# A hybrid SSD, differential-attention and PEER block on one core: ScalarE's queue reordered, and one of four stream buffers turned into a place for gathered rows

## What is computed

```python
hn = rmsnorm(x); z, xbc, dt, q, k, v = split(hn @ w_in)
x = x + concat([ssd(z, xbc, dt), diff_attention(q, k, v)]) @ w_out     # 4 heads, 2 maps a head
xb = rmsnorm(x)                                                        # then PEER
q  = (xb @ w_q).reshape(tokens, 8, 2, 128)
sc = einsum('thjd,hjnd->thjn', q, sub_keys)                            # 8 heads x 2 x 128 keys
idx, g = top-16 of the 256 sums of the two top-16, softmax             # 16 of 16384 experts a head
h  = gelu(einsum('td,thkd->thk', xb, u[idx]))                          # rows of u
x  = x + einsum('thk,thkd->td', g * h, v[idx])                         # rows of v
```

## Time and profile before

| | |
|---|---|
| median of 3 runs | 1404.65 us (1404.16 to 1406.03) |
| profiled execution | 1406.21 us |
| its span | 1403.3 us |
| mean granted clock | 0.995 |
| TensorE, VectorE, ScalarE, GpSimd busy | 1372.8, 1085.2, 435.1, 612.7 us |
| DMA | 467.69 MB, mean 333 GB/s |

### The profile page before, as it was taken

One profiled execution on the slowest core, in us unless ns is written; L12 is line 12 of the kernel. 1 busy time (PEld: TensorE's weight loads), 2 busy tenths in 40 slices (PEclk: granted clock), 3 DMA queues, 4 the chain that ended last, 5 costly groups with the idle time before them and its releaser, 6 DMA issues.

```text
span 1403.3 us, 16312 instructions
## 1 busy us (share of the span) xinstructions
PE 1372.8 (98%) x5402; PEld 937.3 (67%) x5402; DVE 1085.2 (77%) x2469; ACT 435.1 (31%) x1219; POOL 612.7 (44%) x516
## 2 busy tenths in 40 slices
PE   7999999998999999999999999999999999999998
PEld 5656648566488888888899999885444444444443
DVE  4535445898899999999988998998777667765665
ACT  2533532544412121112777887772000000000000
POOL 0000001732855444434457566654577646644440
PEclk9999999999999999999999999999999999999999
DMA  8322334974999999988899999999999999999997
GB/s 304 141 110 105 119 142 176 370 286 162 411 379 408 389 337 378 326 299 320 300 400 378 398 389 383 388 376 366 384 410 409 409 409 409 410 409 409 410 409 313
DMA packets 121619, 467.69 MB, mean 333 GB/s; under 512 B 13760, under 2 KB 14144, under 8 KB 115008
## 3 DMA queue, kind: packets, MB, share of 16 engines
q0 software_dynamic: 73728, 268.47, 49.5%
q1 hardware_dynamic: 47520, 197.66, 36.6%
q10 hardware_dynamic: 288, 0.52, 0.1%
HBM read 462.67 MB, written 3.93 MB: 333 GB/s over the span
## 4 chain that ended last, share of the span: by engine, by line
PE 52%; DVE 24%; DMA 12%; issue 7%; POOL 3%; ACT 2%; SPq 0%; DVEq 0%; ACTq 0%
PE BANKS L944 31%; PE BANKS L722 11%; DMA UV<-v,IDX 8%; DVE X L1611 7%; PE BANKS L714 6%; DMA UV<-u,IDX 4%; POOL UV L1653 3%; DVE BIG L1422 2%; DVE BIG L1606 2%; DVE UV L1606 2%; DVE BIG L1414 2%; DVE BIG L1416 1%; DVE SMALL L1419 1%; DVE BIG L1437 1%; DVE SMALL L1411 1%
## 5 line engine op out<-in xcount | busy, mean ns | idle before, releaser
L1653 POOL DMA_INDIRECT UV<-u,IDX x153 | 187.9, 1228 | 409.9 <-DVE IDX L1483 264.8
L1653 POOL DMA_INDIRECT UV<-v,IDX x159 | 191.5, 1204 | 121.7 <-DVE X L1611 52.9
L1611 DVE SCALAR_TENSOR_TENSOR X<-UV,HG,X 128x1024 f32<-128x1024 f32 x159 | 204.1, 1283 | 39.8 <-DMA UV<-v,IDX 37.3
L920 PE MATMUL BANKS<-T 128*128 128x256 f32 x1024 | 229.1, 379 | 0.0
L944 PE MATMUL BANKS<-T,BIG 128*128 128x512 f32 x512 | 226.9, 596 | 2.0 <-DVE BIG L1627 2.0
L944 PE MATMUL BANKS<-Y,BIG 128*128 128x512 f32 x512 | 225.1, 592 | 0.0
L1606 DVE SCALAR_TENSOR_TENSOR UV<-UV,Y 128x1024 f32<-128x1024 f32 x153 | 186.6, 1223 | 48.7 <-DMA UV<-u,IDX 47.5
L920 PE MATMUL BANKS<-T,Y 128*128 128x256 f32 x992 | 221.9, 379 | 0.0
L920 PEld LDWEIGHTS BANKS<-T 128*128 128x128 f32 x1024 | 192.0, 190 | 24.7
L920 PEld LDWEIGHTS BANKS<-T,Y 128*128 128x128 f32 x992 | 186.0, 190 | 24.0
L944 PEld LDWEIGHTS BANKS<-T,BIG 128*128 128x128 f32 x512 | 97.7, 191 | 125.5 <-issue 122.1
(11 more groups left out here) (272 smaller groups left out, 1248.4 us busy)
## 6 DMA issues: line engine op xcount, KB each, us to landing
T<-u_t SPq DMA_DIRECT2D x64, 512.0 KB, 6.6
T<-v SPq DMA_DIRECT2D x64, 512.0 KB, 6.8
Y<-v SPq DMA_DIRECT2D x64, 512.0 KB, 6.8
Y<-u_t SPq DMA_DIRECT2D x62, 512.0 KB, 6.7
BIG<-w_in SPq DMA_DIRECT2D x23, 1024.0 KB, 6.9
BIG<-w_q SPq DMA_DIRECT2D x16, 1024.0 KB, 8.0
BIG<-w_out SPq DMA_DIRECT2D x8, 1024.0 KB, 6.8
UV<-v,IDX POOLq DMA_INDIRECT x159, 8.2
```

The source lines that it names most:

```text
L920: last = nc.tensor.matmul(PS[(i + 2) % 4][:, 0:HT], ub[:, c, :], T8[:, 1, c, :], start=(c == 0), stop=(c == KC - 1))
L1611: stt(xb, row, HG[:, n % 2, i % UNIT:i % UNIT + 1], xb, ALU.mult, ALU.add).then_inc(used, 1)
L1653: pool.indirect_dma_start(row_place(s), None, u if kind == "ru" else v, bass.IndirectOffsetOnAxis(IDX[:, b, c:c + 1], 0)).then_inc(row_in[ ...
```

## The change

Four things are edited. ScalarE's exponentials become a step `E` of their own for maps 8 to 15 (TensorE and VectorE keep step `A`): E 8 after both first masks, E i+1 after copy B i, E 15 after W 14's copy and ahead of N 2's root. The dense norm F 3 comes before U 2, and ScalarE's copies of key products 6 and 7 (`kc`) after U 3; W 16 and W 17 write banks 2 and 3. `STREAM` loses Y[3], so NS = 3, only load 2 of u goes to X, and load 5 waits for the keys in Y[2]. Y[3] becomes a standing place for gathered rows from row `rows_until(("K", 15)) + 14` on, opened when key product 15 is done.

```diff
     def second_attention(first, end, after, between):
-        out = on("m A", first) + on("m A", first + 1) + between[:1] + on("c", first) + between[1:]
+        out = on("m A", first) + on("m A", first + 1) + on("E", first) + between[:1] + on("c", first) + between[1:]
         for i in range(first, end):
             out += on("B", i)
+            if first < i + 1 < end - 1:
+                out += on("E", i + 1)
             if i + 1 < end:
                 out += on("c", i + 1)
...
             if i == 13:
-                out += then[:1] + on("N", 2) + then[1:2] + on("n2", 2) + on("C", i) + then[2:]
+                out += then[:1] + on("E", 15) + on("N", 2) + then[1:2] + on("n2", 2) + on("C", i) + then[2:]
...
-    after[15] += rows(4) + on("F", 2) + rows(1) + on("R1 Q", 3) + many("K", 4, 6) + on("U", 2) + on("F", 3) + many("K", 6, 8) + on("U", 3) + rows(7)
+    after[15] += rows(4) + on("F", 2) + rows(1) + on("R1 Q", 3) + many("K", 4, 6) + on("F", 3) + on("U", 2) + many("K", 6, 8) + on("U", 3) + many("kc", 6, 8) + rows(7)
...
         STREAM = [T8[:, 0, 0:4, :].rearrange("p c n -> p (c n)"), T8[:, 0, 4:8, :].rearrange("p c n -> p (c n)"),
-                  Y[:, HB, :], Y[:, HB + 1, :]]
+                  Y[:, HB, :]]
...
-            return X[:, j, :] if j in (2, 3) else STREAM[j % NS]
+            return X[:, j, :] if j == 2 else STREAM[j % NS]
...
+                if s == rows_until(("K", 15)) + RING + MORE + 1:
+                    free.append(STANDING)
+                    opened[STANDING] = (ks_full, 16)
...
-        w_bank = lambda i: 0 if PH <= i < 2 * PH else i % 2
+        w_bank = lambda i: 0 if PH <= i < 2 * PH else i % 2 + 2 * (i in (16, 17))
...
-                if j in (2, 3):
+                if j == 2:
                     sp.wait_ge(x_away, 16)
...
-                if j in (6, 7):
-                    sp.wait_ge(ks_full, 12 if j == 6 else 16)
+                if j == 5:
+                    sp.wait_ge(ks_full, 12)
...
-                elif step == "A":
+                elif step == "A" and i < 2 * DH or step == "E":
...
-                elif step == "K":
+                elif step == "kc" or step == "K" and i not in (6, 7):
```

More of the change, by code:

```diff
@@ L391, in block_program @@
         used, h_ready, gelu_done = sem("used"), sem("h_ready"), sem("gelu_done")
-        row_in = [sem(f"row_in{i}") for i in range(RING + MORE)]
+        row_in = [sem(f"row_in{i}") for i in range(RING + MORE + 1)]
         sel_ready, selt_full, selt_done = sem("sel_ready"), sem("selt_full"), sem("selt_done")
@@ L450, in spaces @@
                     for m in range(MORE)]
-        SPACES = spaces()
+        SPACES, STANDING = spaces(), RING + MORE
         LAST_IN = {}
         def ring_places():
-            free, found, count, last_in = list(range(RING)), [], [0] * (RING + MORE), {}
+            free, found, count, last_in = list(range(RING)), [], [0] * (RING + MORE + 1), {}
             left, now, opened = [list(sp) for sp in SPACES], [None] * MORE, {}
             for s, step in enumerate(ROWSEQ):
+                if s == rows_until(("K", 15)) + RING + MORE + 1:
+                    free.append(STANDING)
+                    opened[STANDING] = (ks_full, 16)
                 for m in range(MORE):
@@ L472, in ring_places @@
                 count[k] += 1
-                at = now[k - RING][0] if k >= RING else None
+                at = now[k - RING][0] if RING <= k < STANDING else None
                 found.append((k, count[k], last_in.get(k), at, opened.pop(k, None)))
@@ L489, in row_place @@
             k, _, _, at, _ = PLACES[s]
-            return UV[:, k, :] if k < RING else BIG[:, at:at + DM]
+            return UV[:, k, :] if k < RING else Y[:, HB + 1, :] if k == STANDING else BIG[:, at:at + DM]
         def q_at(half, hj):
@@ L890, in _ @@
                         n = weights_in()
-                    channels(half, j, n, bank_01(w_bank(i), q2_done, i + 1), q2_full,
+                    channels(half, j, n, PS[w_bank(i)] if w_bank(i) > 1 else bank_01(w_bank(i), q2_done, i + 1), q2_full,
                              [(ut_done, 4 * half + 3 + c) for c in range(2)])
```

## The result

The changed kernel took **1432.17 us** (median of 4 runs, 1429.46 to 1436.57), the kernel before 1404.41 (1403.18 to 1406.03) beside it. The ratio is 1.0196, with a 95% interval of 1.0170 to 1.0222: 27.8 us slower. The forecast was 1424.9 in a range of 1405 to 1438, with 0.81 on slower. The direction and the main mechanism came as forecast; one term of the sum, that of the v stream, was 8.5 us too small.

The account below looks back on a forecast made before the run. TensorE, 98% busy, was taken as the bound, with VectorE and full DMA engines close behind. Terms -3.3 - 1.0 - 1.7 + 8 + 6.0 - 1.3 + 13.5 = +20.2 on 1404.65 gave 1424.9 us, range 1405 to 1438.

Parts of the forecast that it names:

- v stream: v products, 987 to 1385 us: three buffers cover 6.65 us of a 6.8 us landing; stalls cost +13.5 us.
- ScalarE's order in attention: Second attention half, 296 to 348 us: moved exponentials cut VectorE's own idle time; -3.3 us.
- Dense norm: 378 to 393 us: F3 before U2, key copies after U3, so W16 starts earlier; -1.0 us.
- Clock after W16: The half-clock stretch after 393 us costs 3.1 us; half of it taken as saved, -1.7 us.
- u stream: u products without one-hots, to 678 us: three buffers leave loads too little time; +8 us.
- Turn: From u to v products: the first v loads go out later and hold TensorE up; +6.0 us.
- sixth place: One more slot for gathered rows from 457 us removes most VectorE waits, little TensorE idling; -1.3 us.
- The part for v3: Within the turn: load v3, issued when v0 is finished, lands too late for its product; +3.6 us.
- The end: TensorE's work in order sets the end; VectorE's gathered rows end 2 us before it.
- Rival A: Loads stay hidden, landing at 6.4 us or less; only the turn costs 1: 1398.4 us, chance 0.13.
- Rival B: Late loads' stalls let TensorE's clock fall to half; +10 to 17 us, some 1438 us, chance 0.12.
- Rival C: Late loads belong only to that trace; v +4, u +3, turn +4: 1408.4 us, chance 0.13.

Follow-up runs that it names:

- h4: Kernel before with four buffers, each u load waiting for one product more; 1411.21 us, ratio 1.0050.
- e1: Kernel before with ScalarE's whole reorder alone (exponentials, dense norm, key copies, banks), four buffers, five standing places; 1400.37 us, ratio 0.9975.
- p1: Kernel before with only ScalarE's exponentials in the new order; 1402.02 us, ratio 0.9998.
- p3: Kernel before with ScalarE's whole reorder, the same kernel as e1 measured again; 1399.86 us, ratio 0.9968.
- p2: Kernel before with only the dense norm's order, the copies of keys 6 and 7 and the banks; 1402.50 us, ratio 1.0003.
- e4: Kernel before with four buffers, each v load from the fifth on waiting for one product more; 1422.55 us, ratio 1.0126.
- e2: Kernel before with three stream buffers, the fourth's place idle, ScalarE's order and five standing places as before; 1433.42 us, ratio 1.0222.
- e3: Changed kernel without the sixth standing place (Y[3] idle); 1433.08 us, ratio 1.0215.
- h3: Changed kernel measured again, nothing altered; 1433.78 us, ratio 1.0200.
- h1: Changed kernel with each 512 KB load of u and v in two 256 KB halves; 1454.42 us, ratio 1.0343.
- h2: Kernel of e1 (four buffers, five places) with each load of u and v in two halves; 1441.60 us, ratio 1.0253.

## Why the prediction was right, and where it was off

- **ScalarE's order in attention, forecast -3.3, measured -2.66.** Near in size, only in part right in cause. h4 splits it: with the old order, but without the half clock at 328, R0 comes 1.4 us sooner; the order itself is worth 1.2. The forecast read VectorE's wait for mask 15 (0.8) and part of the wait for N2's root as ScalarE's order; they were the half clock that follows the 2.56 us gap: in h4, VectorE's waits are 1.8 (one of them) for the maximum's input and 1.2 for N2's root, where the earlier trace rows have 2.6 (two) and 1.8. It counted that clock at nothing, because TensorE does not set the end of this stage; but the slow matmuls feed VectorE. This rests on h4's one trace. VectorE's waits of the changed kernel from 296 to 348 us:

```profile
DVE RS L1569 <- ACT NSQ L1121: 0.9, 1, 0.9
DVE RS L1554 <- ACT BIG L1104: 0.9, 1, 0.9
```

  What was left of the wait for N2's root is 0.9 us, as worked out. The second row, at 298.74, is new: with both masks first, VectorE waits 0.9 us for map 8's exponentials, where the forecast left 0.2. So 4.4 us of waits became 1.8, which is the 2.66. The two gaps of TensorE went as forecast, but gaps of 1.25 (at 340.44) and 1.55 (at 345.43, ahead of R0) took their place.
- **Dense norm, forecast -1.0, measured -0.98.** Right, and the same within 0.02 in all eight traces of the new order.
- **Clock after W16, forecast -1.7, measured -3.1** between these two executions: the midpoint of an open question, and the 3.1 is no fixed price. Over the eight traces of the new order the clock fell in three, and where it fell for 3.4 us, in either order, the 64 records took 15.45 to 15.74, 1.4 to 1.7 more than 14.05; only the profile before had 6.8 us of it.
- **u stream, forecast +8, measured +7.5.** The size is right by luck, by two errors that cancel. The reaction to a landing is 0.34 us, not 0.2 (see the v stream below), which would have made it about 10 with the landings of before; and the landings of the changed kernel are somewhat shorter (median 6.10 for 6.38 over the loads from 457 to 672), which makes it 6.8 to 7.8 in the same replay, as the window is taken.
- **Turn +6.0 and sixth place -1.3, together +4.7; measured +0.8** against the profile of before. That profile is the longest of the kernels with four buffers and whole loads in this stretch, though (288.25; e1, p1, p3, p2, e4, h4 lie at 286.8, 286.0, 284.1, 283.0, 285.3, 283.1); against the mean of those six, 284.7, the changed kernel's two traces are 4.3 and 5.2 longer. The sum is thus near, but its parts are not. The part for v3, +3.6, was wrong: it took 6.8 us of landing where only 3.57 were needed, while the gathers paused. The two waits for v0 and v1 came as described, at 4.7 us where the sum said about 4.4 (2.04 and 2.4).
- **v stream, forecast +13.5, measured +22.0.** This is the step that was mis-sized. The landings were as assumed: median 6.78 us in both kernels, late ones beyond 7.5 us nine times where there had been ten. What failed is the reaction of "about 0.2 more". In the changed kernel's trace 62 of the v products are held up by their load. The first matmul of such a product starts only 0.04 us after the landing, but the second follows it by 0.53 us instead of 0.43, and the last one ends 3.76 us after the landing, where undisturbed products follow each other at 3.43. With the 0.02 until SP's next issue, that is 0.34 us of reaction in the replay's terms, at the median and at the 10th and 90th percentile alike (in e2, e3, e4 and h3 too). The same replay over the landings of before gives 11.9 us at 0.06, 15.9 at 0.2 and 20.9 at 0.35: each 0.1 us costs about 3. I had read the 0.2 off one stall at the turn, which ran half at the slow clock. Fifteen stalls over half a microsecond make 14.5 us, 47 small ones 7.2. The mark-down for "fewer gathers in the last dozen" was right in kind: after 1385.7 only the last load holds TensorE up.
- **The end.** The forecast let TensorE's work set the end, with the rows 2 us short of it. In the kernel before the rows already set it, by about a microsecond (above, e1). For a loss of 28 us that changes little; of a gain of 8 us it took 3.
- **A wait that nobody forecast.** In the changed kernel ScalarE stands for 4.25 us and VectorE for 0.81 until 433.58, and TensorE waits for ScalarE. ScalarE's and TensorE's timelines:

```profile
433.58 1.08 ACT L1171 ACTIVATE BIG<-BANKS 128x512 f32<-128x512 f32 x2 [4.25 <-remote]
```
```profile
434.43 5.94 PE L719 MATMUL BANKS<-T,BIG 128*128 128x256 f32 x20 [3.67 <-ACT BIG L1171]
```

  With 3.4 us of half clock behind it, it costs about 5, and so eats what the clock had given (W16 to gl: +2.0 for the -1.7 of the forecast). It is also in h1, h2 and h3 and, at 1.81 us, in h4, which has none of the change; it is absent in e1, e2, e3, e4, p1, p2, p3 and before. So it is not the change's order by itself. What ScalarE waited for there the profile calls remote and does not name; it stays open.

Rival A (loads hidden) fell with the median landing at 6.78, above the 6.65 at which it decided. So the trace was a better guide than the Trainium skill (DMA: Bandwidth & Descriptors, Anatomy of one DMA), whose sum of a fixed part and bytes over bandwidth gives an estimate of 3.2 us for 512 KB. The page has it for DMAs that GpSimd issues, while this stream is SP's. The trace comes near it only where gathers rest: the 3.57 of v3, and 3.55 at the median from 1387 to 1415. Rival B (half clock after the stalls) fell as well: its time, 1438, is near, but the clock stayed up in the v stage from 985 on (1.00 in the windows), in spite of 14 stalls over half a microsecond; it fell only at the turn, at 966, as it had at 963 before. Rival C (small stalls only) fell; the late loads come in every trace with whole loads (9 to 14 beyond 7.5 us of those issued from 985 to 1385).

The best version found is e1's, the reorder with four buffers: 0.9975 (0.9954 to 0.9996) and 0.9968 (0.9948 to 0.9988) of the kernel before.

## What to carry to other kernels

Count the lead of a prefetch in time and set it against issue to landing plus reaction under the load that will be there: 6.87 against 6.8 + 0.34 is no close call but a loss on half of the products, and here no stall was made good later. When a sum hangs on a tenth of a microsecond repeated a hundred times, measure that tenth on several places of the trace before using it. And look for the second chain: in e1 TensorE gained 8 us and the gathered rows took back 3 of them.

## What the runs showed of the hardware

- From a DMA's landing to the start of the waiting matmul: 0.04 us. The product behind it ends 0.32 us later than it would if it had begun at the landing (3.76 for 3.43), and the next load goes out 0.02 after that; the same in five traces (changed kernel, h3, e2, e3, e4).
- A 512 KB load on SP's queue landed after 6.8 us at the median beside gathers (985 to 1385, all engines full), and after 3.5 to 3.6 once they were over (1387 to 1415; changed kernel 3.55, e2 3.5).
- Two queues on full DMA engines: halving the size of one queue's packets (16703 to 29969 of them in 400 us, e1 and h2) took the total from some 409 to 402 GB/s while both queues were busy, and the loss fell on that queue (60.82 to 54.57 MB), the other kept its 101 to 102 MB.
- A single TensorE gap of 2.08 us was followed by the 1.2 GHz level in three traces and not in five, one of 2.56 us in four and not in a fifth: the length of the last gap alone does not decide it.
